# Moving the down weights of a mixture-of-experts kernel from SyncE's queue to GpSimd's

## The reference, cut to what matters

```python
def expert_block(args):
    xblk, e = args
    hgu = xblk @ w_gu[e] + b_gu[e]              # 1024 x 2048
    gate = jnp.minimum(hgu[:, :D_FF], SWIGLU_LIMIT)
    up = jnp.clip(hgu[:, D_FF:], -SWIGLU_LIMIT, SWIGLU_LIMIT)
    act = gate * jax.nn.sigmoid(SWIGLU_ALPHA * gate) * (up + 1)
    return act @ w_down[e] + b_down[e]          # 1024 x 1024
```

## Time and profile before

| | |
|---|---|
| median of 3 runs | 1143.05 us (1141.73 to 1143.15) |
| profiled execution, its own time | 1143.05 us |
| its span, first to last instruction | 1141.3 us |
| TensorE busy | 1067.8 us, 94% |
| VectorE busy | 414.4 us, 36% |
| ScalarE busy | 173.0 us, 15% |
| GpSimd busy | 2.9 us |
| moved by DMA | 433.18 MB, mean 380 GB/s |

### The profile page before, as it was taken

How to read it: one execution, slowest core, us unless ns; L and a number is a source line. 1 busy time by engine, 2 the same in 40 slices (tenths; PEclk the granted TensorE clock), 3 DMA queues, 4 the chain that set the end, 5 groups by cost and what they waited for, 6 DMA issues and landing times.

```text
span 1141.3 us, 16947 instructions
## 1 busy us (share of the span) xinstructions
PE 1067.8 (94%) x6977; PEld 509.0 (45%) x6977; DVE 414.4 (36%) x716; ACT 173.0 (15%) x295; POOL 2.9 (0%) x12
## 2 busy tenths in 40 slices
PE   2999998699999999999999999999999999999995
PEld 2999964344433333333333434434333333333332
DVE  4366333523333333333333333333333333333344
ACT  4344112211111011011111111111111011001111
POOL 1000000000000000000000000000000000000000
PEclk9899999799999999999999999999999999999998
DMA  9464694799999999999999999999999999999993
GB/s 291 118 185 151 214 397 177 276 430 428 424 431 428 427 431 428 427 430 427 429 388 419 425 427 430 427 429 430 427 429 430 427 428 428 429 428 428 427 424 151
DMA packets 50997, 433.18 MB, mean 380 GB/s; under 512 B 5032, under 2 KB 21952, under 8 KB 25073
## 3 DMA queue, kind: packets, MB, share of 16 engines
q1 hardware_dynamic: 48535, 429.99, 90.9%
q10 hardware_dynamic: 2434, 2.79, 0.8%
HBM read 431.62 MB, written 1.39 MB: 379 GB/s over the span
## 4 chain that ended last, share of the span: by engine, by line
PE 56%; DMA 34%; DVE 4%; issue 3%; ACT 1%; SPq 1%; ACTq 0%; DVEq 0%
DMA down_ring<-in_w_down_dram 20%; PE PS L771 18%; PE PS L797 15%; DMA gu_ring<-in_w_gu_dram 14%; PE PS L627 9%; PE PS L736 3%; PE PS L748 2%; PE PS L679 2%; PE PS L663 1%; PE PS L660 1%; PE PS L749 1%; PE PS L784 1%; PE PS L782 1%; PE PS L811 1%; DVE pick_twice L1114 1%
## 5 line engine op out<-in xcount | busy, mean ns | idle before, releaser
L771 PE MATMUL PS<-gu_ring,XgT 128*64 128x512 f32 x2048 | 471.0, 599 | 9.3 <-DMA gu_ring<-in_w_gu_dram 8.6
L771 PEld LDWEIGHTS PS<-gu_ring,XgT 128*64 128x64 f32 x2048 | 134.3, 136 | 275.4 <-issue 242.3
L797 PE MATMUL PS<-down_ring,actT 128*64 128x512 f32 x992 | 221.7, 596 | 14.0 <-DMA down_ring<-in_w_down_dram 14.0
L1143 DVE TENSOR_TENSOR Y<-PS,Y 128x1024 f32<-128x1024 f32 (+1 forms) x96 | 117.0, 1220 | 267.9 <-PE PS L749 267.9
L1174 DVE SCALAR_TENSOR_TENSOR y_low<-PS,slot_gate,y_high 128x512 fp32r<-128x512 f32 x31 | 23.3, 751 | 310.8 <-ACT y_high L546 310.8
L797 PEld LDWEIGHTS PS<-down_ring,actT 128*64 128x64 f32 x992 | 67.7, 137 | 142.8 <-issue 118.7
L558 ACT ACTIVATE work<-PS 128x512 f32<-128x512 f32 x32 | 19.1, 597 | 471.5 <-PE PS L771 471.5
L627 PE MATMUL PS<-h_high,win_high 128*128 128x264 f32 (+1 forms) x256 | 75.1, 293 | 6.5 <-DVE h_low L930 6.5
L627 PE MATMUL PS<-h_high,win_low 128*128 128x264 f32 (+1 forms) x256 | 74.6, 291 | 0.0
L627 PE MATMUL PS<-h_low,win_high 128*128 128x264 f32 (+1 forms) x256 | 74.5, 291 | 0.0
L736 PE MATMUL PS<-pick,XP 128*128 128x64 bf16 x1792 | 58.6, 194 | 1.0 <-DVE pick L1106 1.0
(11 more groups left out here) (179 smaller groups left out, 659.8 us busy)
## 6 DMA issues: line engine op xcount, KB each, us to landing
gu_ring<-in_w_gu_dram SPq DMA_DIRECT2D x120, 2048.0 KB, 27.0
down_ring<-in_w_down_dram SPq DMA_DIRECT2D x62, 2048.0 KB, 23.1
gu_ring<-in_w_in_dram SPq DMA_DIRECT2D x16, 1024.0 KB, 5.5
gu_ring<-in_w_gu_dram SPq DMA_DIRECT2D x16, 1024.0 KB, 13.1
down_ring<-in_w_o_dram SPq DMA_DIRECT2D x1, 4096.0 KB, 17.4
gu_ring<-in_w_down_dram SPq DMA_DIRECT2D x4, 1024.0 KB, 25.7
gu_ring<-in_w_pool_up_dram SPq DMA_DIRECT2D x1, 2048.0 KB, 7.3
gu_ring<-in_w_conv_out_dram SPq DMA_DIRECT2D x1, 2048.0 KB, 7.5
```

The costliest lines, as they stand in the source:

```text
L771: last = mm(PS[SLOTS * h:SLOTS * h + SLOTS, b, :], XgT[:, k, :], w[:, D * b + HALF * h:D * b + HALF * h + HALF], start=(k == 0), stop=(k = ...
L797: last = mm(PS[SLOTS * h:SLOTS * h + SLOTS, bank, :], acts[:, f % 4, f // 4, :], weights[:, f, HALF * h:HALF * h + HALF], start=(f == 0), ...
L1143: tt(Y[rows, t, :].rearrange("p (h n) -> p h n", h=2), PS[rows, bank:bank + 2, :], Y[rows, t, :].rearrange("p (h n) -> p h n", h=2), ALU.a ...
```

## The change

`load_down` and `item_down` move from the sync block to the gpsimd block, word for word except for the engine. GpSimd waits for the output projection (`wo_done`), loads both halves for item 0, and then runs a loop over items 1 to 30. SyncE keeps the gate-up loads: its two loops become one, in which piece m of item i is issued as soon as item i-2 has used it. The loads of the last item's down weights and of g_final stay on SyncE. The number, the size and the source of all loads, their semaphores and the values waited for are those of before; the work of the other engines is untouched.

```diff
@@ sync block @@
-            for h in range(2):
-                load_down(0, h, False)
...
-            item_gu(2, 2, 0)
-            with sp.Fori(0, AHEAD) as pair:
...
-                item_gu(i + 2, e2, 1)
-                item_down(i, i)
-                item_gu(i + 3, e3, 0)
-                item_down(i + 1, e1)
-            item_down(2 * AHEAD + 1, 2 * AHEAD + 1)
-
-            with sp.Fori(0, E // 2 - 2 - AHEAD) as pair:
...
-                item_gu(i + 1, e1, 1)
-                item_down(i, i)
-                item_gu(i + 2, e2, 0)
-                item_down(i + 1, e1)
-            item_gu(E - 1, E - 1, 1)
-            item_down(E - 2, E - 2)
+            with sp.Fori(0, E // 2 - 1) as pair:
+                i = sp.snap(2 * pair + 2)
+                e1 = sp.snap(2 * pair + 3)
+                item_gu(i, i, 0)
                 item_gu(i + 1, e1, 1)
@@ gpsimd block @@
+            def load_down(e, h, dynamic):
...
+                pool.dma_start(down_ring[:, CH * h:CH * h + CH, :].rearrange("p j n -> p (j n)"), src
+                               ).then_inc(down_landed[h], 16)
+
+            def item_down(i, e):
+                for h in range(2):
+                    pool.wait_ge(down_used, 4 * i + (2 * h - 2))
+                    load_down(e, h, True)
+
+            pool.wait_ge(wo_done, 5)
+            for h in range(2):
+                load_down(0, h, False)
+            with pool.Fori(0, E - 2) as m:
+                i = pool.snap(m + 1)
+                item_down(i, i)
```

More of the change, by code:

```diff
@@ L299, in load_gu @@
                              src).then_inc(gu_landed[CH * parity + m], 16)
[L301 to L306, removed]
             for k in (2, 3, 6, 7):
@@ L326, in _ @@
             load_row(1, 1, 1)
[L328 to L331, removed]
             def item_gu(i, e, parity):
@@ L336, in item_gu @@
                     load_gu(e, parity, m)
-            item_gu(2, 2, 0)
-            with sp.Fori(0, AHEAD) as pair:
[L341 to L344, removed]
-                item_gu(i + 2, e2, 1)
-                item_down(i, i)
-                item_gu(i + 3, e3, 0)
-                item_down(i + 1, e1)
-            item_down(2 * AHEAD + 1, 2 * AHEAD + 1)
-            with sp.Fori(0, E // 2 - 2 - AHEAD) as pair:
-                i = sp.snap(2 * pair + (2 * AHEAD + 2))
-                e1 = sp.snap(2 * pair + (2 * AHEAD + 3))
-                e2 = sp.snap(2 * pair + (2 * AHEAD + 4))
-                item_gu(i + 1, e1, 1)
-                item_down(i, i)
-                item_gu(i + 2, e2, 0)
-                item_down(i + 1, e1)
-            item_gu(E - 1, E - 1, 1)
-            item_down(E - 2, E - 2)
+            with sp.Fori(0, E // 2 - 1) as pair:
+                i = sp.snap(2 * pair + 2)
+                e1 = sp.snap(2 * pair + 3)
+                item_gu(i, i, 0)
+                item_gu(i + 1, e1, 1)
             more = sp.value_load(more_sb[0:1, 0:1], min_val=0, max_val=ROUNDS - 1)
@@ L368, in _ @@
                         e1 = sp.snap(2 * pair + 1)
-                        e_before = sp.snap((2 * pair + (E - 1)) % E)
                         before = sp.snap(r * E + 2 * pair + (E - 1))
-                        item_down(before, e_before)
                         item_gu(before + 1, e0, 0)
-                        item_down(before + 1, e0)
                         item_gu(before + 2, e1, 1)
@@ L406, in _ @@
             nc.gpsimd.tensor_copy(slot_no[:], scr_a.bitcast(I32)[:, 0:2 * SLOTS]).then_inc(consts, 1)
+            def load_down(e, h, dynamic):
+                rows = slice(HALF * h, HALF * h + HALF)
+                src = w_down[0, bass.ds(e, 1), rows, :].rearrange("a (p j) n -> (a p) (j n)", j=CH) \
+                    if dynamic else w_down[0, e, rows, :].rearrange("(p j) n -> p (j n)", j=CH)
+                pool.dma_start(down_ring[:, CH * h:CH * h + CH, :].rearrange("p j n -> p (j n)"), src
[10 more added lines that the diff above has]
+                item_down(i, i)
+            pool.wait_ge(more_ready, 2)
+            more = pool.value_load(more_sb[0:1, 0:1], min_val=0, max_val=ROUNDS - 1)
+            with pool.If(more > 0):
+                with pool.Fori(0, more) as r:
+                    with pool.Fori(0, E) as m:
+                        e = pool.snap((m + (E - 1)) % E)
+                        i = pool.snap(r * E + m + (E - 1))
+                        item_down(i, e)
         @block.scalar
```

## The result

The changed kernel takes 1146.16 us (median of 7 runs, 1144.08 to 1148.07) where the kernel before took 1142.68 (7 runs, 1141.2 to 1143.15): a ratio of 1.0031, with a 95% interval of 1.002 to 1.0042. It is slower by 3.5 us. The forecast was 1146.6 us and +3.5.

The account below looks back on a forecast made before the run. Transfers bound the kernel (29.4 us an item, TensorE 27.4). They end 3.3 us earlier, at 1117.4; 43.4 us of bytes behind gate-up(30) put its step at 1076.0, not 1072.5: 1143.05 + 3.5 = 1146.6 us, range 1141.5 to 1166.5.

Parts of the forecast that it names:

- The hole: Window 595 to 605 us, SyncE's queue stalled between its loops at 285 GB/s: 3.3 us of transfer time, removed by the change.
- The rival of a lower rate: Two active queues move fewer bytes: a 3.3% loss costs 20 us (1166), 1% gives 1152; chance 0.14.
- The share of a half: Queues take turns run by run, so with whole 16 KB rows GpSimd's queue gets half of the engines while both have work.
- The sum: Step k = 6 of item 30 at 1076.0 instead of 1072.5: +3.5 us, with the 3.3 us gain already included.
- The step: Step k = 6 of item 30 waits for its last gate-up piece and starts at 1076.0, before at 1072.54.
- 2 us of landing: Time from a gate-up piece's last byte until TensorE can use it: 2 us.
- tail of down(29): Part of item 29's down weights still to come behind gate-up(30)'s last byte: 3.1 us of transfer, 0.6 pieces.
- steady state: Late items repeat: gate-up last bytes come 29.4 us apart, down traffic at half rate; the tail is worked out from this.
- the prediction's mechanism: Sharing gives gate-up its bytes later, relative to the end of transfers, than the old order did: 6.8 us without the hole's gain.
- The rival of no difference at a share of a third: Down weights take an item's whole 29.4 us, tail 1.1 pieces: +1.1 us, 1144; chance 0.12.
- The starving rival: GpSimd's rows cut into 4 KB packets give down weights a fifth; TensorE waits for them: +23.3 us, 1166 us; chance 0.15.

Follow-up runs that it names:

- warm run: Changed kernel plus four extra products ahead of step k = 6 of items 14 to 27, where TensorE waits: 1146.3 us, ratio 1.0034 to the kernel before.
- run held back by 3.4 us: Changed kernel with the first half of down(i) held back until the second half may go too, 3.4 us later: 1142.75 us, ratio 1.0003.

## Why the prediction was right

**The hole goes and nothing is lost in rate: right.** 424 to 432 GB/s with two queues in every window of 20 us from 240 to 1100, the end of the transfers at 1116.5 where 1117.4 was worked out. The rival of a lower rate is out.

**The share of a half: right, and the term on which the size hangs.** It was read from three landing times of small loads beside w_o. The runs with 16, 8 and 4 KB rows, and the 21.3 us of two halves, bear out turns run by run: a half, a third and a fifth. (Turns of several rows each, as many from either queue, would give the same shares.) Taking turns over the queues is also what the Trainium skill states in "DMA: Bandwidth & Descriptors", section "Queues, rings and completion order", where an engine goes round its queues by packets; the trace agrees with a row of 4, 8 or 16 KB as one packet. The lock of GpSimd by VectorE that the Trainium skill describes ("SBUF — State Buffer", section "SBUF: two separate sides") left no mark that the trace shows: the 62 issues took 0.53 us each, 0.67 at the longest, and TensorE never waited for a half.

**The sum: right in size, and its step by luck.** The step said that step k = 6 of item 30 waits for its last piece and starts at 1076.0. It starts at 1076.3, but it waits for nothing: the piece had landed at 1069.5, 6.8 us earlier. Taking off the prediction's 2 us of landing, its last byte came at 1067.5, and from there to 1116.5 are 10 pieces of 4.9 us, not 8.85. So the tail of down(29) behind it was about 1.75 pieces and not 0.6. down(29) was issued at 1060.45, 21 us behind gate-up(29)'s last byte (1039.4, landed at 1041.4), and the working had 16. That 1076.0 and 1076.3 agree is luck.

What releases the end is item 27's last piece. It lands at 986.9, TensorE has waited 3.58 us for it, and from there it works alone, since the bias products make items 28 to 30 longer than their transfers. The prediction's steady state does hold at that item: it gives a last byte 26.85 pieces of 4.9 us before 1117.4, with landing a start of k = 6 at 987.8, measured 986.99. But I worked this out only afterwards. Before the change the step started at 983.92. The 3.1 us of later landing are the prediction's mechanism; the slower clock behind the wait then adds 1.5 us up to the next down product, and the kernel before loses about 0.9 us of its own in items 28 and 30, so that 3.7 are left in the span.

The mechanism also corrects itself, which the sum did not have: a TensorE that waits issues the next down weights later, and the next gate-up pieces then land earlier. In the changed kernel the waits come in ten items between 13 and 27, not in each; the warm run shows the other direction.

**The tail of down(29): right in sign, too small in size.** I gave 1.7 us for 3.4 us of delay and got 3.2. The traces show two parts. In the run held back by 3.4 us item 27's last gate-up piece lands at 982.5 (issued at 929.1, 53.4 us to landing), 4.4 us earlier than in the changed kernel, so that step k = 6 starts at 983.9 without a wait; and the clock does not fall there, which had cost 1.5 us. The down product starts 4.7 us earlier (991.10 for 995.82), then waits 0.48 us for its second half, and the span is 3.9 us shorter. How the 3.2 us of the medians divide between the two is not shown.

**Not priced.** The falling clock was not in the prediction; by the profile of the warm run it may be worth up to about 1.1 us of the sum. The rival of no difference at a share of a third was wrong in sign of its consequence: it named the tail but not that a half that arrives later than its use turns the order round. The starving rival had the mechanism and far too small a price for 4 KB rows, 23 us for 140; for 8 KB rows and for down weights 4.7 us late its price is nearer (33 and 23 us measured), and for 5.9 us late it is half of the 47 measured.

## What to carry to other kernels

When transfers set the time, putting them on two queues added no bandwidth here (427 to 428 GB/s either way); it changed who comes first, from the order of issue to turns run by run, and the size of a run set the share. Work out which bytes come behind the last one that the compute engine waits for: here a piece or two more or less of them were worth a few microseconds, and a consumer that misses its data by 2 us in each item flips the order for 20 us or more. Look for a hole in the DMA share before changing queues; here one piece issued ahead of one wait gave more than a second queue could.

## What was not expected of the hardware

A load issued from GpSimd in 4 KB rows (512 rows) kept GpSimd's next issue waiting for up to 24.5 us, 46 times and 656 us in all; in the changed kernel, with 16 KB rows, the waits of GpSimd's loads were for TensorE alone.

The length of a wait does not tell whether TensorE's granted clock falls. In the changed kernel eight matmul records behind a wait of 2.36 us took 2.93 us in place of 1.94, and behind one of 3.58 us 3.00; behind one of 3.57 us (at 928.24) they took 1.94. In the warm run the clock fell in a window in which TensorE was busy throughout.
